# A second feed-forward whose gate and value use seven quarter products of sums in place of eight, on half of the contraction, and regrouped GLA matmuls

## The chip, the cores and the metric

One core of a Trainium2 chip runs the whole kernel. The metric is the device time in microseconds (us). TensorE multiplies (PE in the profile; its weight loads are PEld), VectorE is DVE, ScalarE is ACT, GpSimd is POOL, and SP issues most DMAs.

## The reference

Two transformer blocks run one after the other on 256 tokens of width 2048. The change touches the second block's feed-forward and, in the first block, gated linear attention (GLA).

```python
h2 = rms_norm_2(x, g_ffn[i])
x = x + (jax.nn.silu(h2 @ w_gate[i]) * (h2 @ w_up[i])) @ w_down[i]      # width 2048 -> 5632 -> 2048

chunk_update = jnp.einsum('bnhjd,bnhjv->bnhdv', k_to_end, vc)           # GLA: per chunk of 64 tokens
o = o_intra + o_inter            # o_intra = attn @ vc;  o_inter = q_dec @ S_prev
```

## The kernel before

**Units.** All big products run in units. A unit is 512 rows by 512 columns of a weight (four tiles of 128 rows, `KU` = 4, 1 MB). SP loads it into one of four slots of `raw`. ACT copies it to `w_hi` in a reduced format (fp32r), DVE writes the remainder `raw - w_hi` to `w_lo` (`remainder`, L880, or in a loop `remainder_at`, L885), and PE then does three matmuls for each tile and each half of the tokens (`m` = 0, 1): high by high, high by low, low by high. That makes 4 x 2 x 3 = 24 matmuls of 128x512 (`products`, L1506). `w_hi` and `w_lo` have three slots, so ACT can split unit u only once PE has finished unit u - 3 (`unit_used`). The activations are held in the same two parts, `act_hi` and `act_lo`, with the tokens along the free dimension.

**Semaphores.** The order on each engine is the order of the code. Engines wait on counts: `raw_in` (a load has landed), `hi_done`, `lo_done`, `unit_used`, and `acc_free` (a PSUM accumulator has been read). `acc` is two accumulators of two banks (m = 0 and 1), `aux` is four more banks.

**The second feed-forward** (`ffn2` on ACT and DVE, `ffn(1)` on PE) walks over 11 steps of 512 hidden columns. A step has twelve units: four of gate (quarters 0 to 3 of the contraction of 2048), four of value, four of down. In the loop (nine rounds, `FFN_ROUND`) a round is gate of the next step, down of this one, value of the next one. ACT turns the gate accumulator into `gate_tok` with Silu (`gate_silu`), DVE multiplies the value accumulator by it (`up_product`, L1196), PE transposes the product (`f_turn`, L1745), ACT and DVE split it (`f_split`, `f_rest`, L1208), and down's four units are each added to x by DVE (`add_down`, L1216).

**GLA.** `gla_update01` does the updates of chunk 0 for four heads and then of chunk 1 for four heads; a chunk has 64 rows, so each of these matmuls uses half of the array's rows (L1645). `gla_out` does, head by head, one matmul on the whole array (L1670) and then one or two whose output has 64 partitions (L1675).

Of the kernel before, what the change touches and what calls it, by code (L numbers as in the profile page):

```python
# [134 lines left out]
def build_two_blocks(nc, a, out, x_spill):  # L135

    ctx = ExitStack()
    with ctx:
# [82 lines left out]
        gate_tok, val_tok = view(5248, M, N), view(6272, M, N)  # L221
# [47 lines left out]
        last_half, last_stored = sem("last_half"), sem("last_stored")  # L269

# [179 lines left out]
        units += [None] * (12 * FS)  # L450
        G_F2 = G_O2 + 4
        E2 = len(units) - 4
        GD2 = G_F2 + 2 + 6 * (FS - 1)
        for n in range(NG):
            then(E2 + n, "residual", GD2 + n, n, 1)
            then(E2 + n, "square_x", GD2 + n, n)
            then(E2 + n + 2, "turn", 26 + n)
        then(E2 + 1, "turn", 25)
# [3 lines left out]
        embedding(w_pg2, w_pp2, G_P2, 1, 0, DK - 2, 26, 25, 1)  # L462
# [13 lines left out]
        turns += [Turn(xc(n), 4, 1, 4 * n, col_of("g_ffn_2", n), (acc_free, G_O2 + 1 + n)) for n in range(4)]  # L476
        turns += [Turn(p_sb, 2, 0, DK - 2, None, (ple_in[1], 16))]
        turns += [Turn(xc(n), 4, 1, 4 * n, col_of("g_ple_2", n), (acc_free, GD2 + 1 + n)) for n in range(4)]

# [19 lines left out]
        ]  # L499

# [20 lines left out]
        def _(sp):  # L521

            sp.dma_start(ident[:], a["c_ident"]).then_inc(const_in, 16)

            def load(u, src, nk, width):

                if u >= RAW:
                    sp.wait_ge(lo_done, u - RAW + 1)
                sp.dma_start(raw_slot(u % RAW, nk, width), src).then_inc(raw_in[u % RAW], 16)
# [6 lines left out]
            def load_ffn(b):  # L536
                u0 = FFN[b]["u"]
                for n, (kind, q, step) in enumerate(FFN_HEAD):
                    load(u0 + n, ffn_src(b, kind, q, step), KU, N)
                with sp.Fori(0, ROUNDS) as i:  # L540
                    for n, (kind, q, ahead) in enumerate(FFN_ROUND):
                        u = u0 + len(FFN_HEAD) + n
                        sp.wait_ge(lo_done, i * 12 + (u - RAW + 1))
                        sp.dma_start(raw_slot(u % RAW, KU, N), ffn_src(b, kind, q, i + ahead)).then_inc(raw_in[u % RAW], 16)
                for n, (kind, q, step) in enumerate(FFN_TAIL):
                    load(u0 + FT_TAIL + n, ffn_src(b, kind, q, step), KU, N)
# [12 lines left out]
            load_ffn(0)  # L559
            load_units(PL1, F2)  # L560
            load_ffn(1)
# [30 lines left out]
        def _(act):  # L592
            own = Own(act)

            def split(u):

                if u >= UNITS:
                    return
                act.wait_ge(raw_in[u % RAW], 16 * (u // RAW + 1))
# [3 lines left out]
                act.activation(w_hi[:, u % SPL, 0:c], raw[:, u % RAW, 0:c], ACT.Copy).then_inc(hi_done, 1)  # L603
# [23 lines left out]
            def square_pair(src, sums):  # L627
                for m in range(M):
                    if own.last is not None:
                        own.order()  # L630
                    step(ACT.Square, sq_junk, src[:, m, :], squared, accum_out=sums[:, m:m + 1])
# [5 lines left out]
            def square_x(g, n):  # L637
                act.wait_ge(acc_free, g + 1)
                square_pair(xc(n), ssq1[:, n, :])
# [146 lines left out]

            def ffn2():
                u0, g0 = FFN[1]["u"], FFN[1]["g"]
                last = FS - 1
                for j in range(8):  # L790
                    split(u0 + j + SPL)
                    for name, *args in after.get(u0 + j, ()):
                        if name in tasks:
                            tasks[name](*args)
                    if j == 3:
                        gate_silu(g0, 0, u0 + 4)
                with act.Fori(0, ROUNDS) as i:
                    own.enter(i, [(f_hi, 1), (act_step, 1)], (act_step, i + own.n[act_step.num]))
                    for j in range(12):
                        split_at(i, u0 + 8 + j + SPL)  # L800
                        if j == 0:
                            f_split(1, i)
                        if j == 3:
                            gate_silu(i * 6 + (g0 + 2), 0, i * 12 + (u0 + 12))
                    own.leave(ROUNDS, (act_step, own.start[act_step.num] + ROUNDS))
                gt, ut = g0 + G_TAIL, u0 + FT_TAIL
                tail = {0: lambda: f_split(1, last - 1), 3: lambda: gate_silu(gt, 0, ut + 4),
                        8: lambda: f_split(1, last, KU)}
                for j in range(12):
                    split(ut + j + SPL)  # L810
                    if j in tail:
                        tail[j]()
# [54 lines left out]
            walk(lambda u: split(u + SPL), tasks, PL2 - 4, UNITS)  # L867
# [3 lines left out]
        def _(v):  # L871
            own = Own(v)

            def remainder(u):

                if u >= UNITS:
                    return
                v.wait_ge(hi_done, u + 1)
                c = columns(u)
                v.tensor_tensor(w_lo[:, u % SPL, 0:c], raw[:, u % RAW, 0:c], w_hi[:, u % SPL, 0:c],  # L880
                                ALU.subtract).then_inc(lo_done, 1)

# [306 lines left out]
            def up_product(g, slot, used):  # L1189
# [4 lines left out]
                for m in range(M):  # L1194
                    s = acc_free if m == M - 1 else vec_step
                    v.scalar_tensor_tensor(val_tok[:, m, :], acc[:, (slot + FFN[1]["g"]) % 2, m, :], r_col[:, m:m + 1],  # L1196
                                           gate_tok[:, m, :], ALU.mult, ALU.mult).then_inc(s, 1)
                    if m < M - 1:
                        did()
                own.did(acc_free, g + 1)  # L1200
# [60 lines left out]
            def ffn2():  # L1261
                u0, g0 = FFN[1]["u"], FFN[1]["g"]
                last = FS - 1

                def slot(u):
                    if u == u0 + 7:
                        up_product(g0 + 1, 1, u0 + 8)
                    remainder(u + SPL)

                walk(slot, tasks, u0, u0 + 8, first)  # L1270
                with v.Fori(0, ROUNDS) as i:
                    own.enter(i, [(f_done, 1), (vec_step, 1)], (acc_free, i * 6 + (g0 + 2)))
                    for j in range(12):
                        if j == 1:
                            f_rest(1, i)
                        if 4 <= j < 8:
                            add_down(i * 6 + (g0 + j - 1), g0 + j - 1, j - 4, i * 12 + (u0 + 8 + j + 1))
                        if j == 11:
                            up_product(i * 6 + (g0 + 7), 1, i * 12 + (u0 + 20))
                        remainder_at(i, u0 + 8 + j + SPL)  # L1280
                    own.leave(ROUNDS, (acc_free, 6 * ROUNDS + (g0 + 2)))
                ut, gt = u0 + FT_TAIL, g0 + G_TAIL
                for j in range(12):
                    if j == 1:
                        f_rest(1, last - 1)
                    if j == 7:
                        up_product(gt + 1, 1, ut + 8)
                    if j >= 8:
                        add_down(gt + j - 6, gt + j - 6, j - 8, ut + j + 1)
                    if j == 9:  # L1290
                        f_rest(1, last, KU)
                    remainder(ut + j + SPL)
# [179 lines left out]
            walk(lambda u: remainder(u + SPL), tasks, PL2 - 4, UNITS, first)  # L1472
# [3 lines left out]
        def _(pe):  # L1476
# [165 lines left out]
            def update(c, dst):  # L1642
                rows = slice(CH * (c % 2), CH * (c % 2) + CH)
                for h in range(GH):
                    mm = pe.matmul(fours(dst)[:, h, :], k_end_nat[rows, c // 2, GDK * h:GDK * h + GDK],  # L1645
                                   gla_v[rows, c // 2, GDV * h:GDV * h + GDV], start=True, stop=True,
                                   skip_group_check=True)
                return mm

            def gla_update01():  # L1650
# [4 lines left out]
                update(0, aux01)  # L1655
                update(1, aux23).then_inc(upd_full, 1)

            def gla_update2():
                free("01", (state_done, 8))
                update(2, aux01).then_inc(upd_full, 1)  # L1660

            def gla_out(m):
# [4 lines left out]
                for h in range(GH):  # L1667
                    e = slice(GDV * h, GDV * h + GDV)
                    o = fours(dst)[:, h, :]
                    mm = pe.matmul(o, gla_at[:, 2 * h + m, :], gla_v[:, m, e], start=True, stop=False,  # L1670
                                   skip_group_check=True)
# [44 lines left out]
            def ffn(b):  # L1716
                f = FFN[b]
                u0, g0 = f["u"], f["g"]
                turn0 = (6, 21)[b]

                def part(act_b, k0, u, g, flipped, first, last):
                    for k in range(KU):
                        mm = products(act_b, k0 + k, k, u, flipped, g % 2, N, first and k == 0,
                                      last and k == KU - 1)
                    return mm
# [12 lines left out]
                def f_turn(step, g):  # L1738

                    pe.wait_ge(acc_free, g + 1)  # L1740
                    pe.wait_ge(f_done, step + f["it0"])
# [6 lines left out]
                def run(u, kind, q, g, step, i=None, tile=0):  # L1748

                    down = kind == "down"  # L1750
                    if down and q == 0:
                        pe.wait_ge(f_done, step + (f["it0"] + 1))
                    if down or q == 0:
                        pe.wait_ge(acc_free, g - 1 if i is None else i * 6 + (g - 1))
                    pe.wait_ge(lo_done, u + 1 if i is None else i * 12 + (u + 1))
                    if down:
                        mm = part(f["f_act"], tile, u, g, False, True, True)
                    else:
                        mm = part(f["act"], KU * q, u, g, False, q == 0, q == 3)
                    mm.then_inc(unit_used, 1)  # L1760

# [156 lines left out]
```

## Time and profile before

| | us |
|---|---|
| median of 3 runs (2539.12 to 2539.74) | 2539.59 |
| the profiled execution | 2539.72 |
| its span | 2537.6 |
| PE busy | 2521.5 (99%) |
| DVE busy | 1481.1 (58%) |
| ACT busy | 1108.1 (44%) |
| POOL busy | 40.9 (2%) |

The span runs from the first to the last instruction; 2.1 us of the profiled time lie outside it. Busy time is the time in which an engine works on an instruction. Successive matmuls overlap in the records, so that a busy PE is not a measure of its speed; the distance between the starts of two matmuls is. The second feed-forward's loop runs from about 1751 to 2347 us of the span.

### The profile page before, as it was taken

How to read it: one execution, taken by the hardware profiler on the slowest of the kernel's cores; microseconds unless marked ns; L12 is line 12 of the kernel's file. 1: busy time of each engine (PE TensorE's matmuls, PEld its weight loads, DVE VectorE, ACT ScalarE, POOL GpSimd, SP SyncE). 2: the span in 40 equal slices, each digit the busy share in tenths (PEclk: the TensorE clock that was granted, in tenths of full speed). 3: DMA queues.
4: the chain of work that ended last, by engine and by line, in shares of the span. 5: the costliest groups of instructions: out<-in, count | busy, mean ns of one | idle time of the engine just before them, and what ended most of it. 6: DMA issues, size and time to landing. Idle time of an engine off the chain costs nothing.

```text
span 2537.6 us, 29997 instructions
## 1 busy us (share of the span) xinstructions
PE 2521.5 (99%) x12124; PEld 2110.1 (83%) x12124; DVE 1481.1 (58%) x1242; ACT 1108.1 (44%) x1022; POOL 40.9 (2%) x56
## 2 busy tenths in 40 slices
PE   8999999999999999999999999999999999999999
PEld 8988778888888888888888888888888888888887
DVE  5556555566666556667676656554555555555565
ACT  4345434544444444456544433344333333333353
POOL 0000000000000000000000000000000000000000
PEclk9999999999999999999999999999999999999999
DMA  7555465555555555555655555655555556565553
GB/s 266 180 158 171 149 220 183 183 191 189 182 187 193 184 193 185 184 180 179 224 191 185 174 185 195 220 185 194 185 195 185 195 185 198 184 196 184 193 182 121
DMA packets 238100, 476.62 MB, mean 188 GB/s; under 512 B 9974, under 2 KB 10550, under 8 KB 237254
## 3 DMA queue, kind: packets, MB, share of 16 engines
q1 hardware_dynamic: 234390, 460.25, 54.7%
q0 software_dynamic: 3600, 15.25, 1.8%
q8 instruction: 58, 0.95, 0.2%
q14 instruction: 20, 0.16, 0.0%
q10 hardware_dynamic: 32, 0.01, 0.0%
HBM read 471.28 MB, written 4.19 MB: 187 GB/s over the span
## 4 chain that ended last, share of the span: by engine, by line
PE 99%; ACT 0%; DVE 0%; DMA 0%; issue 0%; SPq 0%; ACTq 0%; DVEq 0%
PE acc L1506 88%; PE acc L1499 6%; PE aux L1543 1%; PE aux L1735 1%; PE aux L1745 0%; PE aux L1606 0%; PE aux L1587 0%; PE aux L1685 0%; PE aux L1579 0%; PE aux L1578 0%; DMA mem<-in_x 0%; PE aux L1645 0%; PE aux L1670 0%; PE aux L1675 0%; PE aux L1696 0%; PE aux L1607 0%
## 5 line engine op out<-in xcount | busy, mean ns | idle before, releaser
L1506 PE MATMUL acc<-w_hi,act_hi 128*128 128x512 f32 x3292 | 1290.2, 392 | 0.0
L1506 PE MATMUL acc<-w_hi,act_lo 128*128 128x512 f32 x3292 | 1281.9, 389 | 0.0
L1506 PE MATMUL acc<-w_lo,act_hi 128*128 128x512 f32 x3292 | 1281.1, 389 | 0.0
L1506 PEld LDWEIGHTS acc<-w_hi,act_lo 128*128 128x128 f32 x3292 | 617.8, 188 | 129.4
L885 DVE TENSOR_TENSOR w_lo<-raw,w_hi 128x2048 fp32r<-128x2048 f32 x216 | 495.0, 2292 | 393.4 <-ACT w_hi L609 393.4
L1506 PEld LDWEIGHTS acc<-w_hi,act_hi 128*128 128x128 f32 x3292 | 618.1, 188 | 128.0 <-issue 2.6
L1506 PEld LDWEIGHTS acc<-w_lo,act_hi 128*128 128x128 f32 x3292 | 618.3, 188 | 125.5
L880 DVE TENSOR_TENSOR w_lo<-raw,w_hi 128x2048 fp32r<-128x2048 f32 (+2 forms) x225 | 504.6, 2244 | 362.5 <-ACT w_hi L603 361.9
L609 ACT ACTIVATE w_hi<-raw 128x2048 fp32r<-128x2048 f32 x216 | 414.2, 1918 | 687.5 <-PE acc L1506 687.5
L603 ACT ACTIVATE w_hi<-raw 128x2048 fp32r<-128x2048 f32 (+2 forms) x225 | 422.5, 1878 | 653.8 <-PE acc L1506 587.6
L1216 DVE TENSOR_TENSOR mem<-acc,mem 128x1024 f32<-128x1024 f32 x80 | 98.0, 1225 | 114.5 <-PE acc L1506 114.4
L1499 PE MATMUL acc<-act_hi,w_hi 128*128 128x256 f32 (+1 forms) x400 | 115.8, 290 | 1.9 <-DVE w_lo L880 1.8
L1499 PE MATMUL acc<-act_lo,w_hi 128*128 128x256 f32 (+1 forms) x400 | 114.1, 285 | 0.0
L1499 PE MATMUL acc<-act_hi,w_lo 128*128 128x256 f32 (+1 forms) x400 | 114.1, 285 | 0.0
L1499 PEld LDWEIGHTS acc<-act_hi,w_hi 128*128 128x128 f32 (+1 forms) x400 | 76.3, 191 | 5.6 <-issue 5.2
L612 ACT ACTIVATE mem<-mem 128x512 f32<-128x512 f32 (+1 forms) x86 | 66.7, 775 | 23.5 <-DVE mem L1309 11.2
L1499 PEld LDWEIGHTS acc<-act_lo,w_hi 128*128 128x128 f32 (+1 forms) x400 | 76.3, 191 | 0.4
L1499 PEld LDWEIGHTS acc<-act_hi,w_lo 128*128 128x128 f32 (+1 forms) x400 | 76.2, 190 | 0.3
L1168 DVE SCALAR_TENSOR_TENSOR mem<-aux,conv_now,mem 128x255 f32<-128x255 f32 (+1 forms) x176 | 72.6, 475 | 0.9
L907 DVE SCALAR_TENSOR_TENSOR act_lo<-aux,vec_cols,act_hi 128x256 fp32r<-128x256 f32 x96 | 39.7, 476 | 17.1 <-ACT act_hi L612 17.1
L1817 POOL TENSOR_TENSOR stat<-stat 128x2 f32<-128x2 f32 (+1 forms) x14 | 16.4, 1174 | 2028.8 <-DVE stat L918 1636.2
L966 DVE TENSOR_SCALAR mem<-acc,stat 128x512 f32<-128x512 f32 x40 | 28.2, 747 | 31.3 <-PE acc L1506 29.4
(162 smaller groups left out, 815.4 us busy)
## 6 DMA issues: line engine op xcount, KB each, us to landing
raw<-in_w_in SPq DMA_DIRECT2D x104, 1024.0 KB, 5.2
raw<-in_w_ffn_up SPq DMA_DIRECT2D x88, 1024.0 KB, 5.0
raw<-in_w_ffn_down SPq DMA_DIRECT2D x44, 1024.0 KB, 5.0
raw<-in_w_gate SPq DMA_DIRECT2D x44, 1024.0 KB, 5.2
raw<-in_w_up SPq DMA_DIRECT2D x44, 1024.0 KB, 5.1
raw<-in_w_down SPq DMA_DIRECT2D x44, 1024.0 KB, 5.0
raw<-in_w_ple_gate SPq DMA_DIRECT2D x32, 1024.0 KB, 5.1
raw<-in_w_out SPq DMA_DIRECT2D x16, 1024.0 KB, 5.1
```

Source lines behind the costliest of these rows:

```text
L603: act.activation(w_hi[:, u % SPL, 0:c], raw[:, u % RAW, 0:c], ACT.Copy).then_inc(hi_done, 1)
L609: act.activation(w_hi[:, u % SPL, :], raw[:, u % RAW, :], ACT.Copy).then_inc(hi_done, 1)
L612: act.activation(dst, src, func, **kw).then_inc(sem, 1)
L880: v.tensor_tensor(w_lo[:, u % SPL, 0:c], raw[:, u % RAW, 0:c], w_hi[:, u % SPL, 0:c], ALU.subtract).then_inc(lo_done, 1)
L885: v.tensor_tensor(w_lo[:, u % SPL, :], raw[:, u % RAW, :], w_hi[:, u % SPL, :], ALU.subtract).then_inc(lo_done, 1)
L907: v.scalar_tensor_tensor(lo[:, d.k0 + k, :], fours(half_of[d.half])[:, k, :], d.col[:, k:k + 1], hi[:, d.k0 + k, :].bitcast(F32), ALU.mult ...
L966: v.tensor_scalar(dst[:, m, :], acc[:, g % 2, m, :], r_col[:, m:m + 1], None, ALU.mult).then_inc(s, 1)
L1168: v.scalar_tensor_tensor(dst[:, f, back:T], src[:, f, 0:T - back], conv_now[:, tap, part, f:f + 1], dst[:, f, back:T], ALU.mult, ALU.add). ...
L1216: v.tensor_tensor(xc(n), acc[:, slot % 2, :, :], xc(n), ALU.add).then_inc(acc_free, 1)
L1499: mm = pe.matmul(flat[0:rows, T * f:T * f + T], w[:, c], x[:, k, :], start=start and n == 0 and f % 2 == 0, stop=stop and n == 2, skip_gro ...
L1506: mm = pe.matmul(acc[:, s, m, 0:width], x[:, k, c], w, start=start and n == 0, stop=stop and n == 2, skip_group_check=True)
L1543: mm = pe.transpose(half_of[d.half][:, T * k + P * m:T * k + P * m + P], d.src[:, m, P * k:P * k + P], ident[:])
```

## The change

Ten of the eleven steps of the second feed-forward treat quarters 0 and 1 of gate and value together. Call the activations' four blocks A11, A12 (tokens 0 to 127, quarters 0 and 1) and A21, A22 (tokens 128 to 255), and the weights' blocks B11 (gate, quarter 0), B12 (value, quarter 0), B21 (gate, quarter 1), B22 (value, quarter 1). The eight products of one block with another (12 matmuls each) become seven products `p1` to `p7` of sums: a Strassen scheme in Winograd's form. The sums of activations (`token_sums`, `token_rest`, `sums_split`) are made once, ahead of the loop. The sums of weights (`form`) are made by DVE in each round in place in `raw`, four 128x2048 subtractions. Each of the seven is split and multiplied as a unit of its own, so a round has 15 units, seven of 12 matmuls and eight of 24. Quarters 2 and 3 and down stay whole; down is accumulated in `aux` now, and its units and those of quarters 2 and 3 are loaded into four new buffers (`one_raw`). Since `p1`, `p6` and `p7` add up in one bank (`both`), ACT reads the partial sums out between them (`read_part`), and DVE puts gate and value together (`gate_out`, `pair_out`). The loop has eight rounds, with one round ahead of it and one behind. The GLA matmuls are the same ones in another order: `gla_update01` alternates chunk 0 and chunk 1, `gla_out` does the four whole-array matmuls first.

```diff
+        STEPS2 = ["p1", "p5", ("gate", 2), "p6", ("down", 0), "p7", ("gate", 3), "p2", ("down", 1), "p4", "p3",
+                  ("down", 2), ("value", 2), ("value", 3), ("down", 3)]
+        TAIL2 = ["p1", "p5", ("gate", 2), "p6", ("down", 0), "p7", ("gate", 3), "p2", "p4", "p3", ("value", 2),
+                 ("value", 3), ("down", 1), ("down", 2), ("down", 3)] + [("last", n) for n in range(NG)]
...
+            def split_part(i, u, part, form):
+
+                if form:
+                    act.wait_ge(form_done, times(i, 4, form))
+                else:
+                    act.wait_ge(raw_in[quarter_slot(part)], quarter_count(i, part))
+                act.wait_ge(unit_used, times(i, 15, u - SPL + 1))
+                act.activation(w_hi[:, u % SPL, :], raw[:, quarter_slot(part), :], ACT.Copy).then_inc(hi_done, 1)
...
+            def form(i, dst, a, b, n, after_lo, fresh):
...
+                v.tensor_tensor(quarter(dst), quarter(a), quarter(b), ALU.subtract).then_inc(form_done, 1)
+
+            def form_and_rest(i, u, x, c):
+
+
+                if x == "p1":
+                    form(i, B12, B12, B11, 1, None, (B11, B12))
+                remainder_from(i, u, one_raw[c % 4] if c is not None else quarter(PART_OF[x]))
+                if x == "p5":
+                    form(i, B12, B22, B12, 2, u, (B22,))
+                if x == "p6":
+                    form(i, B11, B12, B11, 3, u, None)
+                if x == "p7":
+                    form(i, B12, B21, B12, 4, u, (B21,))
...
+            def pair_out(i, after_step, b):
+
+
+                v.wait_ge(unit_used, times(i, 15, R2 + after_step + 1))
+                for m in range(M):
+                    v.scalar_tensor_tensor(val_tok[:, m, :], acc[:, 1 - b, m, :], r_col[:, m:m + 1], val_tok[:, m, :],
+                                           ALU.mult, ALU.add).then_inc(pair_done, 1)
+                v.wait_ge(gate_acted, times(i, 1, 1))
+                v.wait_ge(pair_done, times(i, 2, 2))
+                v.tensor_tensor(val_tok, gate_tok, val_tok, ALU.mult).then_inc(val_done, 1)
...
+                def round2(i):
+                    for j in range(15):
+                        if j == 2:
                             f_rest(1, i)
+                        if j in (5, 9, 12):
+                            n = (5, 9, 12).index(j)
+                            add_round2(i, STEPS2.index(("down", n)), n, (aux[:, 0:2, :], aux[:, 2:4, :])[n % 2])
+                        if j == 10:
+                            gate_out(i, STEPS2.index("p4"), b)
+                        if j == 14:
+                            pair_out(i, STEPS2.index(("value", 3)), b)
+                        if j + SPL < 15:
+                            rest2(i, j + SPL)
+                        else:
+                            rest2(i + 1, j + SPL - 15)
+                        if j == 14:
+                            add_round2(i, STEPS2.index(("down", 3)), 3, aux[:, 2:4, :])
...
+                    pe.wait_ge(lo_done, times(i, 15, u + 1))
+                    if x == "p1":
+                        pe.wait_ge(val_done, times(i, 1, 1))
+                        mm = half_product(*quarter(0, 0), u, both, True)
...
             def gla_update01():
...
-                update(0, aux01)
-                update(1, aux23).then_inc(upd_full, 1)
+                for h in range(GH):
+                    update_head(0, aux01, h)
+                    mm = update_head(1, aux23, h)
+                mm.then_inc(upd_full, 1)
```

The first place is DVE at the end of a round of the loop, before the change. The names are tiles; L885 is the remainder of the weights, L1196 the product of value and gate.

```order
L884 REGISTER_ALU
L885 TENSOR_TENSOR w_lo<-raw,w_hi 128x2048 [waits hi_done]
L1192 REGISTER_ALU [waits unit_used]
L1196 SCALAR_TENSOR_TENSOR mem<-acc,stat,mem 128x512 [waits acc_free]
L1196 SCALAR_TENSOR_TENSOR mem<-acc,stat,mem 128x512
L884 REGISTER_ALU
L885 TENSOR_TENSOR w_lo<-raw,w_hi 128x2048 [waits hi_done]
L1271 REGISTER_ALU
L1271 COMPARE_AND_BRANCH
```

The same place after the change: L1056 is the remainder (the first one is that of the next round's `p5`), L1071 the second sum of weights, L1454 and L1458 are `pair_out`, L1465 adds down to x.

```order
L1056 TENSOR_TENSOR w_lo<-raw,w_hi 128x2048 [waits hi_done]
L1066 REGISTER_ALU
L1070 ISA [waits lo_done,raw_in0]
L1071 TENSOR_TENSOR raw<-raw 128x2048 [waits form_done]
L1454 SCALAR_TENSOR_TENSOR mem<-acc,stat,mem 128x512 [waits unit_used]
L1454 SCALAR_TENSOR_TENSOR mem<-acc,stat,mem 128x512
L1457 ISA [waits gate_acted]
L1458 TENSOR_TENSOR mem<-mem 128x1024 [waits pair_done]
L1055 REGISTER_ALU
L1056 TENSOR_TENSOR w_lo<-mem,w_hi 128x2048 [waits hi_done]
L1465 TENSOR_TENSOR mem<-aux,mem 128x2x512 [waits down_added,unit_used]
```

Between a remainder and the reading of the value accumulator there is a subtraction of 2048 columns now, and behind the reading a multiplication of 1024 columns, which was part of L1196 before.

The second place is PE in `gla_out(0)`, before the change; L1670 uses the whole array, L1675 half of its columns.

```order
L1670 MATMUL aux<-mem 128x256 [waits state_done]
L1675 MATMUL aux<-mem 64x256
L1670 MATMUL aux<-mem 128x256
L1675 MATMUL aux<-mem 64x256
L1670 MATMUL aux<-mem 128x256
L1675 MATMUL aux<-mem 64x256
L1670 MATMUL aux<-mem 128x256
L1675 MATMUL aux<-mem 64x256
```

After the change, with the matmuls of the unit that follows (L1799 is `products`):

```order
L1963 MATMUL aux<-mem 128x256 [waits state_done]
L1963 MATMUL aux<-mem 128x256 x3
L1970 MATMUL aux<-mem 64x256 x4
L1799 MATMUL acc<-w_hi,act_hi 128x512 [waits lo_done,acc_free,turned]
L1799 MATMUL acc<-w_lo,act_hi 128x512
```

The eight matmuls are the same; between the two kinds the engine changes once in place of seven times.

## Rows read from the trace of the kernel before

**Rows 1.** The profile's page: busy time per engine, and the chain of work that ended last, by line.
```profile
PE 2521.5 (99%) x12124; PEld 2110.1 (83%) x12124; DVE 1481.1 (58%) x1242; ACT 1108.1 (44%) x1022; POOL 40.9 (2%) x56
...
PE acc L1506 88%; PE acc L1499 6%; PE aux L1543 1%; PE aux L1735 1%; PE aux L1745 0%; PE aux L1606 0%; PE aux L1587 0%; PE aux L1685 0%; PE aux L1579 0%; PE aux L1578 0%; DMA mem<-in_x 0%; PE aux L1645 0%; PE aux L1670 0%; PE aux L1675 0%; PE aux L1696 0%; PE aux L1607 0%
```
**Rows 2.** The chain in order of time, one round: start, us, what.
```profile
1817.74 65.31 PE acc L1506 x288
1883.04 0.87 PE aux L1745 x8
```
**Rows 3.** Busy time of the same round: us, then each engine's, clock, DMA share, GB/s.
```profile
1817.74:1883.92 66.18, 66.18 (x297) 54.89 (x297) 34.96 (x19) 25.08 (x16) 0.00 (x0) 1.00 0.58 190
```
**Rows 4.** Timeline of PE at a unit's end: start us, us, instruction.
```profile
1822.81 0.39 PE L1506 MATMUL acc<-w_hi,act_lo 128*128 128x512 f32 x1
1823.03 0.39 PE L1506 MATMUL acc<-w_hi,act_hi 128*128 128x512 f32 x1
```
**Rows 5.** Timeline of ACT behind that end.
```profile
1823.23 1.92 ACT L609 ACTIVATE w_hi<-raw 128x2048 fp32r<-128x2048 f32 x1 [3.50 <-PE acc L1506]
```
**Rows 6.** Timeline of DVE in that round; in brackets the idle time before.
```profile
1818.85 2.29 DVE L885 TENSOR_TENSOR w_lo<-raw,w_hi 128x2048 fp32r<-128x2048 f32 x1 [3.15 <-ACT w_hi L609]
1821.06 1.22 DVE L1208 TENSOR_TENSOR act_lo<-aux,act_hi 128x1024 fp32r<-128x1024 f32 x1
1825.18 2.29 DVE L885 TENSOR_TENSOR w_lo<-raw,w_hi 128x2048 fp32r<-128x2048 f32 x1 [2.90 <-ACT w_hi L609]
...
1877.79 1.41 DVE L1196 SCALAR_TENSOR_TENSOR mem<-acc,stat,mem 128x512 f32<-128x512 f32 x2 [1.36 <-PE acc L1506]
```
**Rows 7.** Timeline of DVE at a result that its own next instruction waits for.
```profile
1705.03 0.15 DVE L915 TENSOR_REDUCE stat<-stat 128x2 f32<-128x8 f32 x1
1705.22 0.17 DVE L918 TENSOR_SCALAR stat<-stat 128x2 f32<-128x2 f32 x1
```
**Rows 8.** Groups by line and shape: busy us, mean ns of one, idle before.
```profile
L885 DVE TENSOR_TENSOR w_lo<-raw,w_hi 128x2048 fp32r<-128x2048 f32 x216 | 495.0, 2292 | 393.4 <-ACT w_hi L609 393.4
L1186 DVE TENSOR_TENSOR mem<-mem 128x1024 f32<-128x1024 f32 x11 | 13.5, 1225 | 1.1
```
**Rows 9.** The chain in order of time in GLA.
```profile
282.87 2.90 PE aux L1645 x16
...
296.91 1.92 PE aux L1645 x8
...
304.54 0.43 PE aux L1670 x2
304.97 0.57 PE aux L1675 x2
...
309.16 11.10 PE acc L1506 x48
```
**Rows 10.** Timeline of PE in the kernel's first 20 us.
```profile
14.41 0.42 PE L1499 MATMUL acc<-act_lo,w_hi 128*128 128x256 f32 x1
14.63 0.41 PE L1499 MATMUL acc<-act_hi,w_lo 128*128 128x256 f32 x1
...
19.62 0.28 PE L1499 MATMUL acc<-act_hi,w_lo 128*128 128x256 f32 x1
19.74 0.28 PE L1499 MATMUL acc<-act_hi,w_hi 128*128 128x256 f32 x1
```
**Rows 11.** Timeline of PE's last two matmuls.
```profile
2531.28 0.39 PE L1526 MATMUL acc<-w_lo,act_hi 128*128 128x512 f32 x1
2531.51 0.39 PE L1527 MATMUL acc<-w_hi,act_lo 128*128 128x512 f32 x1
```
**Rows 12.** Stretches behind PE's end, columns as in rows 3 (the clock stands third from last).
```profile
2534.00:2535.00 1.00, 0.00 (x0) 0.00 (x0) 0.69 (x1) 0.00 (x0) 0.00 (x0) 1.00 0.69 262
2535.00:2536.00 1.00, 0.00 (x0) 0.00 (x0) 0.00 (x0) 0.00 (x0) 0.00 (x0) 0.54 0.42 160
```
**Rows 13.** What waited for whom in the loop, 1750 to 2345 us: total, times, longest.
```profile
ACT w_hi L609 <- PE acc L1506: 370.0, 108, 3.5
```

More of the change, by code:

```diff
@@ L630, in square_pair @@
                         own.order()
-                    step(ACT.Square, sq_junk, src[:, m, :], squared, accum_out=sums[:, m:m + 1])
+                    step(ACT.Square, junk, src[:, m, :], squared, accum_out=sums[:, m:m + 1])
             def square_first(n):
@@ L794, in ffn2 @@
                             tasks[name](*args)
+                    if j == 2:
+                        sums_split()
                     if j == 3:
                         gate_silu(g0, 0, u0 + 4)
[L797 to L812, printed above, removed]
+                def reads(i, j, steps):
+                    if j == 0:
+                        read_part(i, steps.index("p1"), gate_tok[:, 0, :], both, 0, False)
+                        f_split(1, i)
+                    if j == 1:
+                        read_part(i, steps.index("p5"), val_tok[:, 1, :], cross, 1, True)
+                    if j == 3:
+                        read_part(i, steps.index("p6"), val_tok[:, 0, :], both, 0, True)
+                    if j == 5:
+                        read_part(i, steps.index("p7"), gate_tok[:, 1, :], both, 1, False)
@@ L815, in ple_gate @@
+                last = ROUNDS2 + 1
+                for j in range(15):
+                    split2_tail(j + SPL)
+                    reads(last, j, TAIL2)
+                    if j == 9:
+                        gate_act(last)
+                    if j == 13:
+                        f_split(1, FS - 1, KU)
             def ple_gate(g, n, b):
@@ L1270, in ffn2, with round2 @@
                 walk(slot, tasks, u0, u0 + 8, first)
[L1271 to L1274, printed above, removed]
+                def round2(i):
+                    for j in range(15):
+                        if j == 2:
                             f_rest(1, i)
[L1276 to L1281, printed above, removed]
@@ new lines, in ffn2 @@
+                round2(0)
+                with v.Fori(0, ROUNDS2) as i:
+                    own.enter(i, [(f_done, 1)], (f_done, i + own.n[f_done.num]))
+                    round2(i + 1)
+                    own.leave(ROUNDS2, (f_done, own.start[f_done.num] + ROUNDS2))
+                last = ROUNDS2 + 1
+                at = TAIL2.index
+                for j in range(15):
+                    if j == 2:
+                        f_rest(1, last)
+                    if j == 5:
+                        add_round2(last, at(("down", 0)), 0, aux[:, 0:2, :])
+                    if j == 9:
+                        gate_out(last, at("p4"), b)
+                    if j == 12:
+                        pair_out(last, at(("value", 3)), b)
+                    if j == 13:
+                        add_round2(last, at(("down", 1)), 1, aux[:, 2:4, :])
+                    if j == 14:
+                        f_rest(1, FS - 1, KU)
+                        add_round2(last, at(("down", 2)), 2, acc[:, b, :, :])
+                    rest2_tail(j + SPL)
+                    if j == 14:
+                        add_round2(last, at(("down", 3)), 3, aux[:, 2:4, :])
@@ L1471, in _ @@
             ffn2()
[L1472 removed]
+            walk(lambda u: rest2_tail(u + SPL - T2), tasks, PL2 - 4, UNITS, first)
         @block.tensor
@@ L1640, in gla_scores, with update_head @@
                 mm.then_inc(at_full, 1)
-            def update(c, dst):
+            def update_head(c, dst, h):
                 rows = slice(CH * (c % 2), CH * (c % 2) + CH)
[L1644 to L1648, printed above, removed]
+                return pe.matmul(fours(dst)[:, h, :], k_end_nat[rows, c // 2, GDK * h:GDK * h + GDK],
+                                 gla_v[rows, c // 2, GDV * h:GDV * h + GDV], start=True, stop=True,
+                                 skip_group_check=True)
             def gla_update01():
@@ L1714, in ret_out, with part, run, ffn1 @@
                 mm.then_inc(ret_full, 1)
-            def ffn(b):
-                f = FFN[b]
-                u0, g0 = f["u"], f["g"]
[L1719 to L1725, printed above, removed]
+            def part(act_b, k0, u, g, first, last):
+                for k in range(KU):
+                    mm = products(act_b, k0 + k, k, u, False, g % 2, N, first and k == 0, last and k == KU - 1)
+                return mm
+            def run(b, u, kind, q, g, step, i=None, tile=0):
+                f = FFN[b]
+                down = kind == "down"
+                if down and q == 0:
+                    pe.wait_ge(f_done, step + (f["it0"] + 1))
+                if down or q == 0:
+                    pe.wait_ge(acc_free, g - 1 if i is None else i * 6 + (g - 1))
+                pe.wait_ge(lo_done, u + 1 if i is None else i * 12 + (u + 1))
+                if down:
+                    mm = part(f["f_act"], tile, u, g, True, True)
+                else:
+                    mm = part(f["act"], KU * q, u, g, q == 0, q == 3)
+                mm.then_inc(unit_used, 1)
+            def ffn1():
+                f = FFN[0]
+                u0, g0 = f["u"], f["g"]
                 def up_turn(step, p, g):
@@ new lines, in half_product @@
+            def half_product(x_hi, x_lo, u, o, start):
+                for k in range(KU):
+                    wh, wl = w_hi[:, u % SPL, N * k:N * k + N], w_lo[:, u % SPL, N * k:N * k + N]
+                    pe.matmul(o, x_hi(k), wh, start=start and k == 0, stop=False, skip_group_check=True)
+                    pe.matmul(o, x_hi(k), wl, start=False, stop=False, skip_group_check=True)
+                    mm = pe.matmul(o, x_lo(k), wh, start=False, stop=k == KU - 1, skip_group_check=True)
+                return mm
```

439 lines of the change are left out of this document (346 added, 93 removed).

## The prediction
> **What bounds the kernel now.** I read the page first, then the chain of waits in order of time, the timeline of one round and the waits. PE is busy for 99% of the span and the chain is PE almost throughout, 88% of it in L1506 [rows 1]. A round of the second feed-forward is one unbroken row of 288 matmuls in 65.31 us, 0.2268 us each, and 0.87 us of transposes [rows 2]. DVE is busy for 34.96 us of such a round and ACT for 25.08 [rows 3]. All 108 splits of the loop wait for PE [rows 13], so loads come early enough. The reader is to see that a matmul less on PE is 0.2268 us less, as long as nothing makes PE wait, and that the question is what the change puts in PE's way.
>
> My sum is made against the profiled execution, 2539.72 us (span 2537.6 and 2.1 outside it). The median before is 2539.59.
>
> **What is removed.** Each of ten steps loses one product of 12 matmuls: 120 x 0.2268 = 27.2 us. The seven products add into one bank twelve times running, where L1506 changed banks after three. The last unit of the kernel does that already and its matmuls start 0.23 us apart [rows 11], so I keep the rate.
>
> **What is added beside PE.** A round has three more splits on ACT (1.92 us each [rows 5]) and, on DVE, three more remainders (2.29 us [rows 8]), four `form` subtractions and the new read-outs. By the rows DVE comes to 15 x 2.29 + 4 x 2.29 + 4 x 1.22 (down) + 4 x 0.70 (`gate_out`, `pair_out`) + 2 x 1.22 = 53.6 us, ACT to some 34. A round of 276 matmuls is 62.6 + 0.87 = 63.5 us, so both fit, and as loads stay at 12 MB a round they do too (58% share [rows 3]). The `form` instruction does not occur before: it reads and writes f32 at 2048 columns. The nearest row is L885 at 2.29 us. Twice the 1024-column f32 row (1.225 [rows 8]) would be 2.45. I take 2.29. The sums of activations before the loop (about 9 us of DVE and ACT) fall in units of 5.44 us where DVE works about half the time, and three units are split ahead. I cost them at nothing; without that cover they would cost once, up to 2 us.
>
> **The wait that is added.** `p1` of the next round writes the bank `both`, which holds half of value's result. So PE waits there for `val_done`, which comes at the end of `pair_out`. Behind PE's wait stands its whole queue. On DVE `pair_out` stands behind the remainder of the next round's `p5` and the `form` after it, as the order of DVE in the change shows. And `p5` can be split only when value's last unit is done, since it takes that unit's slot of `w_hi`. So one chain starts with the end of value's last unit, and PE has only down's last unit to do meanwhile. Let S be the first matmul of that down unit.
>
> - ACT starts the split at S + 0.20 (1823.03 to 1823.23 [rows 4, 5]) and DVE the remainder at S + 2.15 (1825.18 [rows 6]).
> - `form` needs that remainder's end: 2.29, and 0.04 for a result that the engine itself waits for (1705.03 + 0.15 to 1705.22 [rows 7]): S + 4.48.
> - The first read-out follows without such a wait 2.21 later (1818.85 to 1821.06 [rows 6]): S + 6.69. Two of them take 1.41 [rows 6]: S + 8.10.
> - The multiplication starts 0.04 later and takes 1.23 [rows 8]: S + 9.37. With 0.04 to reach PE: S + 9.41.
>
> PE would be ready at S + 24 x 0.2268 = S + 5.44. It waits 3.97 us, more than the 2.72 that the round has saved. There are nine such boundaries: 35.7 us. At the first, from the head, the chain has no multiplication behind it (`up_product` does both): S + 8.14, a wait of 2.7 us. In the tail the transposes of the tenth step wait with one unit as cover for a chain without `form`: 2.15 + 2.21 + 1.41 + 0.04 + 1.23 + 0.04 = 7.08, less 5.44, 1.6 us. Together 40.0 us. A DVE operation slower than its row enters in full: `form` at 2.45 would add 9 x 0.16 = 1.4 us; at the shortest, if each hop between engines cost nothing, the boundary would be 3.7 us and the sum 2.5 us less.
>
> I walked the rest of the round in the same way. PE finds its remainder early at each other unit; the margin is least at down's second unit, about 1.0 us, and at down's first, 1.7 us for `f_rest`.
>
> **GLA.** PE is on the chain there too. Sixteen records of L1645 take 2.90 us and eight take 1.92 [rows 9]: the second eight, on the other half of the array's rows, cost 0.98, since part of them ran beside the first. Alternated, I let all pairs overlap: 1.92, a gain of 1.0. In `gla_out(0)` a whole-array matmul takes 0.43 at first and a half-column one behind it 0.57, and the four pairs take 309.16 - 304.54 = 4.62 [rows 9]. Without the changes between kinds: 4 x 0.43, 0.57 and 3 x 0.43 = 3.6, a gain of 1.0, and again 1.0 in `gla_out(1)`. Together -3.0. The bounds: if pairs of halves don't overlap better than now, -2.0; if each alternation cost the 0.14 between 0.57 and 0.43, seven of them would take back 1.0 more: -1.0.
>
> **TensorE's clock.** A wait of 3.97 us inside dense work has no like in this trace. The nearest row stands at the end: PE's last matmul ends at 2531.9 [rows 11], the granted clock is still 1.00 from 2534 to 2535 and 0.54 from 2535 to 2536 [rows 12], so it fell at about 2535.1, some 3.2 us after the work had ended. A stop of 4 us is longer than that. What a fall costs shows at the start: from 14.06 us on PE works without a gap, its 256-column matmuls start 0.22 apart at 14.4 and 0.12 apart at 19.6 [rows 10], the two levels of 1.2 and 2.4 GHz. Those 5.4 us at half speed are 5.4 x (1 - 0.12/0.213) = 2.4 us lost (0.213 is the steady distance there). One observation doesn't say how often a stop of 4 us would be caught. The bounds are none of the nine (0 us) and all nine (21.6 us). I take three, 7.2 us, because the stop outlasts the 3.2 us by a quarter only.
>
> The Trainium skill ("TensorE: Matmul & The Clock Gate", "Why this matters for your kernels") warns against idle gaps between bursts of matmuls in mid-kernel, as they bring the lower clock back. It speaks against this change: by it every one of the nine gaps would count, and the sum would be 2571; by a clock that holds it would be 2549.5. The trace agrees that idleness lowers the clock, and can't say whether each gap does.
>
> **The sum.** 2539.7 - 27.2 + 40.0 - 3.0 = 2549.5, and 7.2 for the clock: 2556.7. Against the median, 2556.6.
>
> **Rivals.**
> 1. *The clock holds or falls once:* 2549.5 to 2552. For it: no stop is longer than 4.0 us. Against it: rows 12.
> 2. *The clock falls at nearly all boundaries:* seven to ten falls at 2.4, 2566 to 2573. For it: the same rows 12, if the fall needs less than full idleness; the first boundary, 2.7 us, may then count too. Against it: each PE stop is only just long enough.
> 3. *The wait is hidden, and the kernel is faster.* The place is `pair_out` in DVE's order. If `val_done` came before PE gets to `p1`, nothing of the 27.2 us would be given back: 2539.7 - 27.2 - 3.0 = 2509.5. It decides at a chain of S + 5.44 for the full gain, and the kernel breaks even near S + 8.3, where the nine waits are 2.9 each (27.2 + 3.0 - 2.7 - 1.6 = 25.9). The chain is S + 9.41 by the rows, and no instruction in it is a guess except `form`, which would have to take 1.2 us or less. Against it stands the f32 row of 1225 ns for half the columns, so I give it little.
> 4. *DVE becomes the bound within the round.* With `p1`, `p5`, `p6` and `p7` lasting 2.72 us on PE and asking 4.58 us of DVE each (remainder and `form`), the margin of 1.0 us at down's second unit is gone if DVE's operations are 3 to 5% longer among the denser traffic. Each 0.5 us beyond it is 5 us in ten rounds, on top of the forecast: 2560 to 2568. Against it: L885 has a mean of 2292 ns over 216 instances, so it hardly varies.
>
> **How the numbers follow.** Forecast (stop of 4 us, two to six falls): 0.42, its own range 2552 to 2564. Rival 1: 0.22. Rival 2: 0.20. Rival 4: 0.07. Rival 3, in full or in part: 0.05 faster and 0.04 within 0.2%, which is 5.1 us and about what a measurement here can tell from no change. The range leaves out rival 3 and the end of rival 2: 2547 to 2569. Faster 0.05, same 0.04, slower 0.91.
>
> **What would show it.** On PE, one idle stretch of about 4.0 us in each of nine rounds, ahead of the first matmul of `p1`, ended by DVE's multiplication (L1458), and none elsewhere above 0.3 us but the 2.7 and the 1.6. The distance from one `p1` to the next: 67.5 us at full clock against 66.2 before. The clock row in stretches of a round: 1.00 for a round without a fall, about 0.96 with one. L1071 at a mean near 2290 ns. In GLA, the first group at 1.9 us and each `gla_out` at 3.6. I am wrong if L1458 ends before down's last unit does, if the rounds are shorter than 66 us, or if PE waits for `lo_done` inside a round.

## The result, and the profile after

| | us |
|---|---|
| before, median | 2539.58 |
| changed, median of 4 runs (2572.97 to 2574.41) | 2573.44 |
| ratio | 1.0135, 95% interval 1.0123 to 1.0148 |
| the changed kernel's profiled execution, and its span | 2572.97, 2570.7 |

The change made the kernel slower by 33.9 us, on the forecast side, but 16.8 us more than forecast and beyond the range.

First the page after: busy time per engine, then the chain by engine, and the clock in forty slices. They answer to [rows 1].

```profile
PE 2514.6 (98%) x12004; PEld 2101.7 (82%) x12004; DVE 1662.5 (65%) x1348; ACT 1189.8 (46%) x1083; POOL 41.1 (2%) x56
...
PEclk9999999999999999999999999999999999999999
...
PE 95%; DVE 3%; ACT 1%; issue 1%; DMA 0%; DVEq 0%; SPq 0%; ACTq 0%
```

PE has 120 matmuls fewer, but the chain leaves PE for 5% of a longer span, and goes over DVE and ACT there. The clock's slices of 64 us show nothing: a digit 9 is anything from 0.9 up. The waits of PE say where (who waited for whom: total, times, longest):

```profile
PE acc L2082 <- DVE mem L1458: 35.8, 9, 4.1
PE aux L1836 <- DMA mem<-in_x: 5.2, 2, 2.8
PE aux L2218 <- DMA ident<-c_ident: 2.8, 1, 2.8
PE acc L2082 <- DVE mem L1408: 2.7, 1, 2.7
PE aux L2118 <- DVE mem L1458: 1.6, 1, 1.6
```

The first row is the nine boundaries, the fourth the head, the fifth the tail; the two between are the kernel's start, and the trace before has the same two waits (5.2 and 2.9 us). The chain in order of time at the first boundary (start, us, what) has the forecast's links, one after the other; it answers to [rows 2, 4 to 6].

```profile
1800.94 3.41 PE acc L1799 x15
1804.43 1.92 ACT w_hi L699
1806.38 2.30 DVE w_lo L1056
1808.77 2.29 DVE raw L1071
1811.06 1.33 DVE mem L1454 x2
1812.48 1.24 DVE mem L1458
1813.76 0.58 PE acc L2082
1814.34 0.43 PE acc L2083
1814.77 0.43 PE acc L2084
...
1817.33 0.34 PE acc L2084
1817.67 0.23 PE acc L2082
```

PE stands still from 1809.6 to 1813.76. The reader is to see the last rows: when PE goes on, its 512-column matmuls start 0.43 us apart, and from 1817.67 again 0.23. That is the lower clock of 1.2 GHz after the stop. The same at all nine boundaries, in stretches of 10 us around each (us, busy time of PE, PEld, DVE, ACT, POOL, the granted clock, DMA share, GB/s):

```profile
1812.00:1822.00 10.00, 8.24 (x33) 6.76 (x34) 6.59 (x5) 3.41 (x3) 0.00 (x0) 0.83 0.32 107
1881.00:1891.00 10.00, 7.95 (x27) 6.42 (x28) 5.78 (x6) 2.46 (x4) 0.00 (x0) 0.66 0.30 105
1952.00:1962.00 10.00, 8.40 (x34) 6.87 (x35) 6.66 (x5) 3.54 (x4) 0.00 (x0) 0.83 0.29 105
...
2370.00:2380.00 10.00, 8.14 (x29) 6.59 (x30) 5.66 (x5) 2.59 (x3) 0.00 (x0) 0.66 0.30 105
```

No boundary is spared: five read 0.83 and four 0.66. In the head, where PE stopped for 2.9 us, the stretch from 1744.4 to 1750 reads 0.70, so that stop was caught too. The forecast had three falls.

GLA came out as forecast. The chain there after, against [rows 9]:

```profile
282.35 1.93 PE aux L1937 x16
...
303.05 1.73 PE aux L1963 x8
304.77 1.87 PE aux L1970 x8
306.64 11.11 PE acc L1799 x48
```

2.90 us became 1.93, and 4.62 became 3.59. In `gla_out(1)` the two groups take 1.73 and 1.88 us, 3.61 in place of 4.64.

### The profile page after: what moved, and what is told of

Read it like the earlier page. It is cut to its first block, busy times and chain, and to the rows that moved or that the text cites. A ratio compares the mean times of both kernels' runs of the same rounds, so it can differ in the third digit from the quotient of the medians.

```text
span 2570.7 us, 30099 instructions
## 1 busy us (share of the span) xinstructions
PE 2514.6 (98%) x12004; PEld 2101.7 (82%) x12004; DVE 1662.5 (65%) x1348; ACT 1189.8 (46%) x1083; POOL 41.1 (2%) x56
## 4 chain that ended last, share of the span: by engine, by line
PE 95%; DVE 3%; ACT 1%; issue 1%; DMA 0%; DVEq 0%; SPq 0%; ACTq 0%
PE acc L1799 69%; PE acc L1792 6%; PE acc L2082 3%; PE acc L2084 3%; PE acc L2083 3%; PE aux L2083 2%; PE aux L2084 2%; PE aux L2082 2%; PE aux L1836 1%; DVE w_lo L1056 1%; PE aux L2043 1%; ACT w_hi L699 1%; DVE mem L1454 1%; DVE mem L1458 0%; PE aux L2118 0%
## 5 line engine op out<-in xcount | busy, mean ns | idle before, releaser
L1799 PE MATMUL acc<-w_hi,act_hi 128*128 128x512 f32 x2620 | 1027.6, 392 | 0.0
L1799 PE MATMUL acc<-w_hi,act_lo 128*128 128x512 f32 x2620 | 1020.3, 389 | 0.0
L1799 PE MATMUL acc<-w_lo,act_hi 128*128 128x512 f32 x2620 | 1019.6, 389 | 0.0
L1799 PEld LDWEIGHTS acc<-w_hi,act_lo 128*128 128x128 f32 x2620 | 491.8, 188 | 103.2
L1799 PEld LDWEIGHTS acc<-w_hi,act_hi 128*128 128x128 f32 x2620 | 492.0, 188 | 102.0 <-issue 2.6
L1799 PEld LDWEIGHTS acc<-w_lo,act_hi 128*128 128x128 f32 x2620 | 492.2, 188 | 99.7
L1056 DVE TENSOR_TENSOR w_lo<-raw,w_hi 128x2048 fp32r<-128x2048 f32 x70 | 160.4, 2292 | 122.0 <-ACT w_hi L699 122.0
L1056 DVE TENSOR_TENSOR w_lo<-mem,w_hi 128x2048 fp32r<-128x2048 f32 x84 | 192.0, 2286 | 57.2 <-ACT w_hi L705 57.2
L705 ACT ACTIVATE w_hi<-mem 128x2048 fp32r<-128x2048 f32 x84 | 161.2, 1919 | 131.8 <-PE aux L2084 77.5
L2082 PE MATMUL acc<-w_hi,act_hi 128*128 128x512 f32 x320 | 134.1, 419 | 38.7 <-DVE mem L1458 35.8
L2084 PE MATMUL acc<-w_hi,act_lo 128*128 128x512 f32 x320 | 132.4, 414 | 0.0
L2083 PE MATMUL acc<-w_lo,act_hi 128*128 128x512 f32 x320 | 132.0, 413 | 0.0
L2082 PE MATMUL aux<-w_hi,act_hi 128*128 128x512 f32 x312 | 121.4, 389 | 0.0
L2083 PE MATMUL aux<-w_lo,act_hi 128*128 128x512 f32 x312 | 121.4, 389 | 0.0
```

The source lines that it names most:

```text
L705: act.activation(w_hi[:, u % SPL, :], one_raw[c % 4], ACT.Copy).then_inc(hi_done, 1)
L1056: v.tensor_tensor(w_lo[:, u % SPL, :], src, w_hi[:, u % SPL, :], ALU.subtract).then_inc(lo_done, 1)
L1799: mm = pe.matmul(acc[:, s, m, 0:width], x[:, k, c], w, start=start and n == 0, stop=stop and n == 2, skip_group_check=True)
L2082: pe.matmul(o, x_hi(k), wh, start=start and k == 0, stop=False, skip_group_check=True)
L2083: pe.matmul(o, x_hi(k), wl, start=False, stop=False, skip_group_check=True)
L2084: mm = pe.matmul(o, x_lo(k), wh, start=False, stop=k == KU - 1, skip_group_check=True)
```

## The experiments

Each kernel was timed against the kernel before on the same chip. Where nothing else is said, a round is the distance between two transposes L2118 of neighbouring rounds.

**1. The order of DVE.** The nine stops, if they come from the place of `pair_out` alone, should go when it moves ahead of the next round's `p5`.

```diff
-                        if j == 14:
+                        if j == 13:
                             pair_out(i, STEPS2.index(("value", 3)), b)
```

> Edit: in the rounds of the loop DVE does pair_out before the remainder of the next round's p5 and the second sum of weights, not behind them; nothing else is moved. Theory A (the nine stops ahead of p1 come from this order of DVE alone, and the lower clock comes from the stops): val_done comes 2.9 us after value's last unit ends, so PE does not wait at the nine boundaries. The 37 us of stops and nine of the ten falls of the clock go; what stays is the first boundary (2.9 us and one fall) and the 1.8 us in the tail. The changed kernel's 2573.4 less 37 and less 9 x 2.2 = 2516.5. Theory B (DVE is short of time in the round whatever its order, 53.6 us of work in 63.5): the wait moves to the remainders of p5 or gate's unit, PE waits there 1 to 4 us a round, and the time is 2530 to 2560. Theory C (the clock falls because of the denser work of all engines in this stage, not because PE stops): falls stay in each round, and the time is about 2536.

Measured: 2515.85 us, ratio 0.9909 (0.9893 to 0.9924). All that PE waited for between 1700 and 2510 us:

```profile
PE acc L2082 <- DVE mem L1408: 2.7, 1, 2.7
PE aux L2118 <- DVE mem L1458: 1.6, 1, 1.6
PE acc L2082 <- DVE act_lo L1473: 0.2, 1, 0.2
```

The nine stops are gone, and the timeline of DVE at a boundary shows how: the read-outs and the product stand ahead of the remainder now, and the sum of weights (L1071) behind it.

```profile
1804.14 1.41 DVE L1454 SCALAR_TENSOR_TENSOR mem<-acc,stat,mem 128x512 f32<-128x512 f32 x2 [1.05 <-PE acc L1799]
1805.66 1.23 DVE L1458 TENSOR_TENSOR mem<-mem 128x1024 f32<-128x1024 f32 x1
1806.80 2.29 DVE L1056 TENSOR_TENSOR w_lo<-raw,w_hi 128x2048 fp32r<-128x2048 f32 x1
1809.18 2.29 DVE L1071 TENSOR_TENSOR raw<-raw 128x2048 f32<-128x2048 f32 x1
```

The busy time of a whole stretch of the loop, PE without a break, and the clock at 1.00:

```profile
1754.00:2360.00 606.00, 606.00 (x2712) 502.46 (x2711) 498.70 (x276) 317.09 (x203) 0.00 (x0) 1.00 0.57 194
```

A round is 1875.73 - 1812.27 = 63.46 us, the 63.5 of the forecast's sum. DVE works 82% of it and still binds nowhere, so theory B falls. One fall would not show in the mean of 606 us, but in a mean of 67 us it would: the changed kernel's round from 1814 to 1883, which has one, reads 0.97. All nine stretches of 67 us from 1753 to 2356 read 1.00. The engines are denser here than in the changed kernel and the clock stays up, so theory C falls. The head keeps its stop of 2.9 us and its fall (0.83 from 1740 to 1750).

**2. Half of the way.** With `pair_out` between the remainder and the sum of weights the stop is shorter by one subtraction.

```diff
                 remainder_from(i, u, one_raw[c % 4] if c is not None else quarter(PART_OF[x]))
+                if between is not None:
+                    between()
                 if x == "p5":
                     form(i, B12, B22, B12, 2, u, (B22,))
...
+                        elif j == 13:
+                            rest2(i + 1, j + SPL - 15, lambda: pair_out(i, STEPS2.index(("value", 3)), b))
```

> Edit: in the rounds of the loop DVE does pair_out behind the remainder of p5 but before the second sum of weights. Theory A: the stop ahead of p1 shrinks by one subtraction and its own wait, from 4.1 to 1.8 us. The time without any change of the clock at the nine boundaries is 2573.4 - 9 x 2.33 - 9 x 2.2 = 2532.6; if a stop of 1.8 us still lowers the clock each time it is 2552. As the tail's stop of 1.8 us in the changed kernel was not followed by a fall, I expect 2532 to 2535. Theory B: no more than half of the stop goes, over 2555 us. Theory C: falls in each round, 2552.

Measured: 2531.34 us, ratio 0.997 (0.9958 to 0.9982). PE's waits in the loop, and stretches of 10 us around two of the nine boundaries:

```profile
PE acc L2084 <- DVE mem L1460: 13.5, 9, 1.6
```
```profile
1870.00:1880.00 10.00, 8.53 (x43) 6.81 (x42) 8.87 (x6) 3.89 (x3) 0.00 (x0) 1.00 0.00 0
1935.00:1945.00 10.00, 8.52 (x43) 6.81 (x41) 8.61 (x6) 3.89 (x3) 0.00 (x0) 1.00 0.00 0
```

By PE's starts seven stops are 1.6 us and two are 1.7 and 1.8. All nine stretches read 1.00, so no fall at any of them. The time is the one that was expected for a clock that holds, 1.3 us lower still. The head has its stop of 2.9 us and its fall here too.

**3. The price of the clock by itself.** PE does useless matmuls in the stop, so that it waits as long as before but is not idle.

```diff
                     if x == "p1":
+                        if later:
+                            pe.wait_ge(down_added, times(i, 4, -1))
+                        for n in range(16 if later else 10):
+                            pe.matmul(aux[:, 0, :], quarter(0, 0)[0](n % KU), w_hi[:, u % SPL, 0:N], start=True,
+                                      stop=True, skip_group_check=True)
                         pe.wait_ge(val_done, times(i, 1, 1))
```

> Edit: the changed kernel with 16 more matmuls of 128x512 ahead of each wait of p1 for val_done (10 ahead of the first), into a bank that is free at that time and whose result nobody reads; they take 3.6 us of the 4.1 us for which PE stands still, so they can't lengthen a round. Theory A (two prices: the stop, and the clock that falls because of it): the clock stays at 2.4 GHz throughout, the round becomes 67.6 us from one p1 to the next, and the time is 2573.4 - 22 = 2551. Theory C: the clock falls as before and the time stays at 2573. If the falls were without price (PE's slow matmuls hidden by the chain over ACT and DVE), the time also stays at 2573 although the clock holds.

Measured: 2553.11 us, ratio 1.0054 (1.0039 to 1.007). The timeline of PE at the first boundary (L2130 are the useless ones), and the clock over the stage:

```profile
1808.43 3.79 PE L2130 MATMUL aux<-w_hi,act_hi 128*128 128x512 f32 x16
1812.58 0.50 PE L2082 MATMUL acc<-w_hi,act_hi 128*128 128x512 f32 x1 [0.36 <-DVE mem L1458]
1812.91 0.40 PE L2083 MATMUL acc<-w_lo,act_hi 128*128 128x512 f32 x1
```
```profile
1700.00:2460.00 760.00, 754.77 (x3380) 622.23 (x3379) 578.56 (x340) 374.33 (x268) 2.74 (x4) 1.00 0.55 187
```

`p1` starts when DVE's product is done, as in the changed kernel, but at full clock. Each of ten stretches of 72 us from 1739 to 2459 reads 1.00, the head's among them. More matmuls, 20.3 us less (2573.44 - 2553.11). That is the clock's whole price, ten falls of 2.0 us in the mean. A round is 67.79 us here (1883.41 - 1815.62), 67.6 was expected; against the 63.46 of experiment 1 the nine stops as such cost nine times 4.3, some 39 us. The times differ by less, 37.3 us (2553.11 - 2515.85), since experiment 1 still has the head's fall and this kernel has none.

**4. GLA alone**, in the kernel before.

```diff
+                for h in range(GH):
+                    update_head(0, aux01, h)
+                    mm = update_head(1, aux23, h)
...
+                for h in range(GH):
+                    mm = pe.matmul(fours(dst)[:, h, :], gla_at[:, 2 * h + m, :], gla_v[:, m, GDV * h:GDV * h + GDV],
+                                   start=h % 2 == 0, stop=False, skip_group_check=True)
```

> Edit: the kernel before with the new order of GLA's matmuls alone. By the traces of before and after, the first group goes from 2.90 to 1.93 us and each gla_out from 4.6 to 3.6, and PE is on the chain there: 3.0 us less, 2536.6. Rival: the gain is given back later because ACT or DVE bind behind it: 2539.6.

Measured: 2536.31 us, ratio 0.9988 (0.9979 to 0.9997), 3.0 us less by the medians. The interval alone allows 0.8 to 5.3 us; the chain is closer, with 0.97 and two times 1.03 us less at the three places. The group of sixteen reads 1.93 us and half-column groups 1.87 and 1.88, as in the changed kernel; nothing of it is given back. The matmuls are the same but for one flag: `start` is set for every second whole-array matmul only, where it was set for each.

**5 and 6. How long a stop it takes.** The sum of weights ahead of `pair_out` is cut to 1024 and to 512 of its 2048 columns, to have stops between 1.6 and 4.1 us. The rest of that sum is left out.

```diff
-                    form(i, B12, B22, B12, 2, u, (B22,))
+                    form(i, B12, B22, B12, 2, u, (B22,), 1024)
```

The diff is that of experiment 5; the new last argument is the number of columns, and experiment 6 has 512 there.

> Edit: the changed kernel, but the second sum of weights in each round (the one ahead of pair_out) subtracts only 1024 of its 2048 columns; this leaves half of that sum out. The stop ahead of p1 becomes 4.1 - 1.07 = 3.1 us, the first one 1.8. What is asked is whether a stop of 3.1 us still lowers the clock. If in each round (the first stop of the changed kernel, 2.9 us, was followed by a fall): 2573.4 - 9 x 1.07 - 1.1 - 2.2 = 2560.5. If in none: 2540.7. If it is caught only now and then, in between.

> Edit: the same with 512 of the 2048 columns subtracted; this leaves three quarters of that sum out. The stop becomes 4.1 - 1.6 = 2.5 us. With a fall in each round 2555.6, with none 2535.8. A stop of 1.6 us had no fall in ten of ten, one of 2.9 had one in one of one, so I hold some falls for likely: 2540 to 2550, three to six of them.

Measured: 2556.79 us (ratio 1.0069, 1.0052 to 1.0085) and 2547.09 us (1.0031, 1.0017 to 1.0045). With 1024 columns the nine stops are 3.1 us and each of the nine stretches of 7 us around them reads 0.76. With 512 columns they are 2.5 us, and six of nine do. Of the latter's nine rows, four:

```profile
1808.00:1815.00 7.00, 5.12 (x26) 4.31 (x27) 5.13 (x5) 3.52 (x3) 0.00 (x0) 1.00 0.20 63
1874.00:1881.00 7.00, 4.97 (x17) 3.98 (x18) 5.28 (x5) 1.94 (x2) 0.00 (x0) 0.76 0.17 50
1942.00:1949.00 7.00, 5.25 (x21) 4.19 (x21) 5.00 (x4) 1.93 (x2) 0.00 (x0) 0.76 0.21 63
2009.00:2016.00 7.00, 4.64 (x25) 3.81 (x25) 5.74 (x5) 3.34 (x2) 0.00 (x0) 1.00 0.08 20
```

The first time is 3.7 us lower than I expected from nine falls at 2.2 us: behind a stop of 3.1 us a fall costs 1.6 (a round is 68.27 us, and 63.46 + 3.06 + 0.15 would be 66.67). The 0.15 is what a stop costs beside its length. It shows in experiment 2, where a round is 65.25 us and the stop 1.64 (65.25 - 63.46 - 1.64). The first matmuls behind a stop start 0.33 and 0.24 us apart, not 0.227, and a few later ones of `p1` 0.24 or 0.23. All nine rounds of experiment 5 have the same timing: they are 68.27 us long, and in each the clock falls 0.1 us after PE has gone on. So its nine falls are one case nine times, and not nine independent ones. The second lies within what I expected, with the upper end of the falls.

**7. A version that beats both.** Experiment 1, and besides it the tail's `pair_out` ahead of the remainder of down's last unit, and the head's `up_product` ahead of the second sum of weights.

```diff
+                    elif u == u0 + 6:
+                        rest2(0, 1, lambda: up_product(g0 + 1, 1, u0 + 8))
...
-                    if j == 12:
+                    if j == 11:
                         pair_out(last, at(("value", 3)), b)
```

> Edit: pair_out ahead of the remainder of p5 in the loop (as in the run that did this alone), and besides pair_out of the tail ahead of the remainder of down's last unit, and in the head up_product ahead of the second sum of weights. Theory A: the tail's stop of 1.8 us goes, the head's shrinks from 2.9 to 1.8 and is then too short for a fall of the clock: 2515.9 - 1.8 - 1.1 - 1.6 = 2511.4. Rival: the fall of the clock in the head is not due to the stop, then 2513.

Measured: 2511.35 us, ratio 0.989 (0.9873 to 0.9906), 28.2 us below the kernel before and 62.1 below the changed one. PE's waits from 1700 to 2510, and the clock around the head:

```profile
PE acc L2084 <- DVE mem L1410: 1.6, 1, 1.6
PE acc L2084 <- DVE act_lo L1475: 0.2, 1, 0.2
```
```profile
1740.00:1760.00 20.00, 18.41 (x85) 14.98 (x85) 16.89 (x10) 11.19 (x8) 0.00 (x0) 1.00 0.59 207
```

The tail's stop is gone, the head's is 1.8 us by PE's starts and no longer followed by a fall (one in these 20 us would read about 0.91).

## Why the prediction was wrong

The direction and the mechanism were right, and one term of the sum was mis-sized. By its own steps:

- *Removed matmuls, -27.2 us: right.* With the stops out of the way a round is 63.46 us (experiment 1) against 66.20 before [rows 2].
- *Cost beside PE nothing: right.* DVE's work in a round was forecast at 53.6 us, is 52.2 in experiment 1 (498.70 x 63.46 / 606) and was covered. L1071 has a mean of 2289 ns, the 2.29 that was taken. The sums of activations ahead of the loop delayed nothing: PE waits for no remainder in any of these kernels' loops.
- *The added wait, +40.0 us: right in place and chain, slightly low.* By PE's starts a boundary is 4.13 us, not 3.97, since three links took 0.06 more each: ACT's start, the subtraction and the multiplication (1806.38 to 1808.77 is 2.39, not 2.33). The restart of PE costs 0.15 besides. Nine times 0.16 + 0.15 is 2.8 us.
- *GLA, -3.0 us: right* (experiment 4).
- *The clock, "I take three, 7.2 us, because the stop outlasts the 3.2 us by a quarter only": the step that failed.* There were ten falls of ten stops above 2.5 us, for 20.3 us (experiment 3). I had read the 3.2 us between PE's end and the lower clock [rows 11, 12] as a time that a stop has to outlast, and so held falls for rare. The experiments show that it is no such bound: stops of 2.5 us were caught six times in nine, and in the changed kernel's head the clock was still up when PE went on at 1744.46 and fell 1.3 us later. In all nine rounds of experiment 5 it fell after PE had gone on, too. One observation at the kernel's end told how late a fall may come, not how short a stop may be.

With 20.3 in place of 7.2 and 2.8 for the stops' own excess the sum is 2539.7 - 27.2 + 42.8 - 3.0 + 20.3 = 2572.6, against 2573.0 in the profiled run. Rival 2 (nearly all boundaries, 2566 to 2573) had the mechanism, at 0.20; its price of 2.4 us for one fall was too high by a fifth. The warning of the Trainium skill ("TensorE: Matmul & The Clock Gate", "Why this matters for your kernels") against idle gaps between bursts agrees with the changed kernel's trace at every boundary, where the gaps are 4.1 us. Not every gap counts: none of the nine of 1.6 to 1.8 us in experiment 2 was followed by a fall. I gave the single row more weight than the rule. Rival 3 named the right place for a gain and its size: the order of DVE, and 2509.5 with the waits hidden. It was wrong for this kernel and right for experiments 1 and 7, at 2515.85 and 2511.35. Rival 4 did not occur.

My range left this out: it stopped at 2569 and gave up "the end of rival 2", though that rival was one in five and its own numbers went to 2573.

## What to carry to other kernels

When work moves from a saturated engine to one with idle time, the sum of busy times says nothing of the engine's waits: write down what stands in the second engine's queue between the last input and the result that the first one waits for, and put that result first. Here the same instructions cost 58 us more with a remainder and a subtraction ahead of the read-out than behind it. And price each stop of TensorE in two parts, its length and the slow matmuls behind it: in these runs stops of up to 1.8 us were never followed by a fall, stops of 2.5 us were in six rounds of nine, and stops of 2.9 us and more always. A stop of 2.5 us or more that is repeated in each round of a loop should be counted as caught unless a run shows otherwise.

## What the runs showed of the hardware that I had not expected

| stop of PE, us | stops | clock fell | kernel |
|---|---|---|---|
| 1.6 to 1.8 | 9 | 0 | experiment 2, loop |
| 1.8 | 9 | 0 | tail of the changed kernel and of experiments 1, 2, 3, 5 and 6; head of 5, 6 and 7 |
| 2.5 to 2.6 | 9 | 6 | experiment 6 |
| 2.9 | 3 | 3 | head of the changed kernel and of experiments 1 and 2 |
| 3.1 | 9 | 9 | experiment 5 |
| 4.1 to 4.2 | 9 | 9 | changed, loop |

- Between 1.8 and 2.9 us the share of falls goes from none to all. At 2.5 us it is a matter of the round: with the same stop three rounds kept 2.4 GHz. Which rounds these are was not explained by a run. Why the same stop is followed by 0.83 in some rounds of the changed kernel and 0.66 in others was not tried.
- Useless matmuls in a stop made the kernel 20.3 us faster (experiment 3). It is no cure where the stop itself can go, since that gave 57.6.
- Matmuls on different halves of the array's rows hid each other almost wholly when they alternated in the queue, and only in part when they were grouped by half: eight records more cost 0.98 us grouped [rows 9] and 0.01 alternated (1.93 against 1.92).
